# Down-projections of a squared-ReLU MLP as seven block products instead of eight, with their weight sums formed in HBM by the DMA queue

## The chip, the cores and the metric

The kernel runs on one core of one Trainium2 chip, as one launch. The metric is the device time of a launch in microseconds (us), the median of several runs. In the profile PE is TensorE, DVE is VectorE, ACT is ScalarE, POOL is GpSimd and SP is SyncE.

## What is computed

One layer of a hybrid decoder for 1088 tokens (a prompt of 1024 and 8 samples of 8): token mixers, cross-attention, then the MLP to which the change belongs, and a final norm. All is in float32.

```python
hm = _rmsnorm(x, g_mlp)
x = x + jnp.square(jax.nn.relu(hm @ w_up)) @ w_down   # (T, 1024) @ (1024, 4096), then (T, 4096) @ (4096, 1024)
y = _rmsnorm(x, g_final)
```

## The kernel before

**Number format.** Each float32 operand of a large product is kept as a high part (rounded to the matmul's format, fp32r) and a low part (the rest), and each product is three matmuls: high by high, high by low, low by high. Of every weight tile POOL makes the high part (the cast at L509, `msp<-mraw`) and DVE the low part (`unit_lo`, `msp<-mraw,msp`). Of the activations ACT makes the high part and DVE the low part.

**The MLP.** The hidden width of 4096 is worked through in eight stretches (d = 0, 1 of four groups o). A stretch has two quads (q) of 256 hidden rows each: the up-projection of a quad, and after both the down-projection of their 512 hidden rows into all 1024 outputs, which is added to the residual `F`. The first group and the last are written out, the middle two are a loop of two trips (`pair_loop`, L410).

**A quad** is already a block product with seven multiplications (`ORDER`, `PRODUCTS`): a product is 24 matmuls of 272 columns (`product`, L1293), its weight tile is one unit of 128x512 (an up-block of `w`, or a sum of blocks from the tensor `sums_up` in HBM). DVE combines the results (`Quad.c11`, `c22`, `c12`, `c21`), applies ReLU and scale (`squeezed`), ACT squares (`squared`) and makes the high part, DVE the low part (`hidden_lo`). The first stretch has an order of its own (`opening`).

**A down-projection** (`down`, L1368) has 8 output tiles of 128 rows, one weight unit each. A tile is 4 (contraction) x 3 (parts) x 3 (column pieces of 364, 364 and 360) = 36 matmuls, 288 in the stretch. Two sets of three PSUM banks take turns. DVE adds each tile to `F` in one instruction of 1092 columns.

**The weight sums.** Four sums per group (S1 to S4) for the up-projections are formed in HBM by DMAs that POOL issues, 32 steps of 1024 KB (`sum_step`, L471): `put` copies, `plus` adds while writing. One step follows each of the first 32 weight slots that POOL splits for the input projections (`split`, L442); slots 0 to 13 belong to the plain projections, slots 14 to 31 to the filling, where PE puts input-projection work between steps of the recurrence.

**What sets the order.** Every engine runs the order that its block writes out, tied by counting semaphores. In this program's rows some appear under the name of an earlier use: `as_tc` is m_used (PE has used a unit), `as_nm` is m_hi (POOL has cast a unit), `as_tp` is m_ready (its low part is there), `at_tc` is m_lo (low parts of the hidden activations), `at_ox` is m_f (reads of PSUM into `F`), `at_mx`, `at_ex`, `at_nm` are m_b, m_c, m_z (blocks of a quad), `at_tp` is m_sq (squares), `rg_t` is t_hi, `as_oc` is m_half, `o_dve` is DVE's wait for itself.

## Time and profile before

| | |
|---|---|
| median of 3 runs | 2252.41 us (2246.67 to 2255.57) |
| the profiled execution | 2245.91 us |
| its span, first to last instruction | 2244.1 us |
| PE busy | 2182.6 us (97%) |
| DVE busy | 1065.8 us (47%) |
| ACT, POOL busy | 533.4, 440.1 us |
| mean granted clock of PE | 0.996 |
| DMA queue of POOL (q0) | 12800 packets, 33.56 MB, 6.9% of 16 engines' span |

The span is divided into the input projections (to about 250 us), the recurrence with filling and the mixers, attention, and the MLP (from 1490 us to the end). Matmuls are pipelined in PE, so a matmul's own duration overlaps the next one; the spacing of starts is what it costs.

### The profile page before, as it was taken

The page shows a single profiled execution, that of the slowest core. Times are in us where ns is not written, and L with a number is a line of the kernel's source. Part 1 is how long each engine was busy: PE and PEld are TensorE (multiplying, and loading weights), DVE is VectorE, ACT ScalarE, POOL GpSimd, SP SyncE. Part 2 cuts the span into 40 slices and gives each one's busy share as a digit, 9 for nine tenths or more (in the row PEclk, how much of TensorE's full clock was granted, in tenths as well). Part 3 has the DMA queues.
Part 4 walks back from the last instruction along what each step waited for, and adds up shares of the span by engine and source line. Part 5 has one row for each costly group of instructions (what it writes and reads, how often), then busy time and mean ns, then how long its engine had stood idle before and what let it go on. Part 6 is the DMA issues. An engine that isn't in the chain of part 4 may idle for free. (4 is left out here: it accounts for less than half of the span.)

```text
span 2244.1 us, 49247 instructions
## 1 busy us (share of the span) xinstructions
PE 2182.6 (97%) x21418; PEld 2061.6 (92%) x21418; DVE 1065.8 (47%) x1526; ACT 533.4 (24%) x1014; POOL 440.1 (20%) x368
## 2 busy tenths in 40 slices
PE   8999999999999999999999999998999999999997
PEld 6899888888888899989999987998999999999997
DVE  5333643636445355263544155466445445354455
ACT  4111433324333221153011023231102011011023
POOL 0233301112021022122333200321111111111110
PEclk9999999999999999999999999999999999999999
DMA  8446513424053074336113125111212122122122
GB/s 306 144 129 137 142 39 82 89 54 149 7 114 70 27 244 162 105 135 254 47 40 119 47 96 187 38 57 62 70 53 76 57 67 72 52 76 64 55 76 80
DMA packets 86663, 217.61 MB, mean 97 GB/s; under 512 B 10720, under 2 KB 26464, under 8 KB 83680
## 3 DMA queue, kind: packets, MB, share of 16 engines
q1 hardware_dynamic: 62944, 156.22, 21.0%
q0 software_dynamic: 12800, 33.56, 6.9%
q10 hardware_dynamic: 10752, 25.35, 3.2%
q8 instruction: 137, 2.24, 0.4%
q14 instruction: 30, 0.25, 0.0%
HBM read 187.04 MB, written 61.60 MB: 111 GB/s over the span
## 5 line engine op out<-in xcount | busy, mean ns | idle before, releaser
L517 PE MATMUL ps<-A_s,w_split 128*128 128x364 f32 (+1 forms) x3888 | 693.5, 334 | 1.9 <-ACT zstg L2250 1.9
L517 PEld LDWEIGHTS ps<-A_s,w_split 128*128 128x128 f32 x3888 | 643.5, 188 | 28.1 <-issue 12.5
L517 PE MATMUL ps<-hid,msp 128*128 128x364 f32 (+3 forms) x2304 | 388.3, 330 | 5.4 <-issue 5.4
L517 PEld LDWEIGHTS ps<-hid,msp 128*128 128x128 f32 x2304 | 385.1, 189 | 7.3 <-issue 6.0
L449 POOL CAST w_split<-w_raw 128x1024 fp32r<-128x1024 f32 x78 | 85.5, 1096 | 1117.0 <-PE ps L517 858.0
L517 PE MATMUL ps<-B_s,w_split 128*128 128x364 f32 (+1 forms) x1728 | 288.1, 328 | 0.4 <-POOL w_split L451 0.4
L517 PEld LDWEIGHTS ps<-B_s,w_split 128*128 128x128 f32 x1728 | 286.7, 188 | 0.7 <-issue 0.7
L1434 DVE TENSOR_TENSOR F<-ps,F 128x1092 f32<-128x1092 f32 (+3 forms) x84 | 104.3, 1241 | 352.3 <-PE ps L517 352.3
L509 POOL CAST msp<-mraw 128x512 fp32r<-128x512 f32 x176 | 115.1, 655 | 616.6 <-PE ps L517 604.0
L451 POOL TENSOR_TENSOR w_split<-w_raw,w_split 128x1024 fp32r<-128x1024 f32 x78 | 206.9, 2652 | 6.3
L517 PE MATMUL ps<-xb,msp 128*128 128x272 f32 x1536 | 200.2, 288 | 1.5 <-DVE F L1434 1.5
L517 PEld LDWEIGHTS ps<-xb,msp 128*128 128x128 f32 x1536 | 195.9, 188 | 1.8 <-issue 1.8
L517 PE MATMUL ps<-xt,msp 128*128 128x272 f32 x1152 | 152.2, 288 | 1.5 <-DVE xt L1434 1.0
L517 PEld LDWEIGHTS ps<-xt,msp 128*128 128x128 f32 x1152 | 147.4, 188 | 2.1 <-DVE xt L1434 1.2
L1434 DVE TENSOR_TENSOR msp<-mraw,msp 128x512 fp32r<-128x512 f32 x176 | 121.2, 690 | 51.6 <-POOL msp L509 49.7
L2250 ACT ACTIVATE hidf<-ps 128x544 f32<-128x544 f32 x32 | 20.0, 626 | 383.2 <-PE ps L517 383.2
L1434 DVE TENSOR_TENSOR pdf<-prw 128x1024 f32<-128x1024 f32 x14 | 40.9, 2919 | 99.3 <-ACTq L2354 99.3
L2250 ACT ACTIVATE hid<-hidf 128x544 fp32r<-128x544 f32 x64 | 42.2, 660 | 190.9 <-DVE hidf L1440 190.9
L2250 ACT ACTIVATE zstg<-ps 128x364 f32<-128x364 f32 x96 | 45.3, 474 | 173.4 <-PE ps L517 130.0
L1434 DVE TENSOR_TENSOR hidf<-ps,hidf 128x544 f32<-128x544 f32 x62 | 44.9, 724 | 42.0 <-PE ps L517 42.0
L1434 DVE TENSOR_TENSOR Xst<-ps,msk 128x256 f32<-128x256 f32 (+1 forms) x88 | 35.8, 407 | 53.7 <-PE ps L517 52.0
L1434 DVE TENSOR_TENSOR F<-F 128x384 f32<-128x384 f32 (+2 forms) x64 | 43.9, 697 | 25.3 <-ACT F L2250 24.7
(249 smaller groups left out, 2408.4 us busy)
## 6 DMA issues: line engine op xcount, KB each, us to landing
w_raw<-w SPq DMA_DIRECT2D x80, 512.0 KB, 3.7
mraw<-w SPq DMA_DIRECT2D x112, 256.0 KB, 2.6
sums_up<-w POOLq DMA_DIRECT2D x24, 1024.0 KB, 9.4
mraw<-sums_up SPq DMA_DIRECT2D x64, 256.0 KB, 2.6
z<-zstg SPq DMA_DIRECT2D x83, 182.0 KB, 2.1
F<-z SPq DMA_DIRECT2D x16, 546.0 KB, 7.1
sums_up<-sums_up POOLq DMA_DIRECT2D x8, 1024.0 KB, 5.9
w_raw<-w SPq DMA_DIRECT2D x7, 1024.0 KB, 10.3
```

Of the source, the lines that this page charges most:

```text
L449: pool.tensor_copy(ws[:, b, 0, :, :], raw[:, b, :].rearrange("p (k n) -> p k n", k=KT)).then_inc(w_hi, 1)
L451: pool.tensor_tensor(ws[:, b, 1, :, :], raw[:, b, :].rearrange("p (k n) -> p k n", k=KT), w32, ALU.subtract).then_inc(w_ready, 1)
L509: pool.tensor_copy(msp[:, l % 4, 0, :, :], mraw[:, l % 4, :].rearrange("p (k n) -> p k n", k=4)).then_inc(m_hi, 1)
L517: return pe.matmul(out, lhsT, rhs, start=start, stop=stop, skip_group_check=skip)
L1434: return v.tensor_tensor(out, a, b, op)
L2250: return a.activation(out, in_, f, **k)
```

## The change

**Down-projections.** Six of the eight stretches, all but (o, d) = (0, 0) and (3, 1), take seven block products. The weight block is 1024 outputs x 512 hidden, cut in even and odd output tiles, two halves of 256 hidden rows (the two quads) and two halves of 544 tokens. A product has 4 output tiles, 2 contraction tiles, 3 parts and 2 column pieces of 272: 48 matmuls, 336 in the stretch. It takes two units (`FAST` lists 14), and each half of a unit's work ends in a tile that DVE reads into `F` (`read`, 544 columns, 28 a stretch). Four of the seven products use weight sums, from a new HBM tensor `sums_down`. The hidden operands must be combined too: `tf = H11 - H12`, `H12 - H22`, `tf + H22`, and two more, with their high parts by ACT (`turned_hi`) and low parts by DVE (`turned_lo`, `lower`). In these stretches DVE's low parts of 544 columns per quad are partly dropped and partly replaced.

**Residual.** Through these six stretches `F` holds its blocks in another basis; two DVE instructions of 2176 columns bring it in (after quad 2 of group 0) and two bring it back (after quad 2 of group 3): `residual_in`.

**Opening and first down-projection.** DVE's order at the end of `opening` is changed, and PE's first down-projection (`down_first`) goes through its first two tiles one contraction step at a time, with a wait for each.

**Weight sums.** 64 steps instead of 32, two after each of the first 32 slots. The 32 new ones form `sums_down`: 1024 KB in groups 1 and 2 (where a `plus` is two DMAs), 512 KB in groups 0 and 3. That makes 72 DMAs.

**Smaller edits.** A stretch has 14 units instead of 8; unit numbers run through the program (`mlp_units`, `mlp_ring`). One accumulator moves from banks 3 and 4 to banks 2 and 3. POOL's loop over slots is written out. SP's wait for all sums stands just ahead of the MLP's loads.

```diff
+        FAST = [(p, u) for p in (1, 2, 7, 3, 5, 4, 6) for u in range(2)]
+        UNITS_BEFORE, READS_BEFORE = {0: 0, 1: 50, 3: 162}, {0: 0, 1: 36, 3: 148}
+        def mlp_fast(o, d):
+            return (o, d) not in ((0, 0), (3, 1))
...
-            for n in range(XT + SIDE):
+            done = 0
+            for n in range(S_MLP - S_PW):
                 split(n, n % 2)
-                if n < 32:
-                    sum_step(n)
+                for _ in range(2 if n < 32 else 0):
+                    if done < 32:
+                        sum_step(done, 0, sum_block, up_block)
+                    else:
+                        sum_step(done - 32, 8, down_sum, down_block)
+                    done += 1
...
+            def down_first():
+                r = [mlp_ring(0, down_unit(0, 0, t)) for t in range(2)]
                 for t in range(2):
+                    pe.wait_ge(m_ready, mlp_units(0, 0, down_unit(0, 0, t) + 1))
+                    pe.wait_ge(m_lo, mlp_lows(0, 0, 0, 2))
+                    pe.wait_ge(m_b, BEFORE + 5 + t)
+                    down_part(r[t], t, (0,))
+                for k, n in ((2, 4), (1, 6), (3, 8)):
+                    pe.wait_ge(m_lo, mlp_lows(0, 0, 0, n))
+                    for t in range(2):
+                        last = down_part(r[t], t, (k,))
...
+            OPERAND = {1: (0, 0), 2: (1, 0), 7: (0, 1), 3: (1, 1), 5: (0, 0), 4: (1, 0), 6: (0, 0)}
+            NEED = {1: 1, 2: 3, 7: 4, 3: 6, 5: 5, 4: 7, 6: 8}
+            def down_fast(i, o, d):
+                n = 4 * o + 2 * d + 2
+                for s, (p, u) in enumerate(FAST):
+                    l = down_unit(o, d, s)
+                    v, h = OPERAND[p]
+                    if u == 0:
+                        pe.wait_ge(m_lo, mlp_lows(i, o, d, NEED[p]))
+                    pe.wait_ge(m_ready, mlp_units(i, o, l + 1))
+                    for j in range(2):
+                        t = 2 * u + j
+                        if s >= 2:
+                            pe.wait_ge(m_f, mlp_reads(i, o, d, 4 * (s // 2 - 1) + t + 1))
...
+                        for k in range(2):
+                            for m, (wp, xp) in enumerate(((0, 0), (0, 1), (1, 0))):
+                                for c in range(2):
+                                    x0 = HT * h + HC * c
+                                    last = mm(ps[:, 2 * t + c, 0:HC], msp[:, mlp_ring(o, l), wp, 2 * j + k, :], hid[v][:, k, xp, x0:x0 + HC],
...
+                        last.then_inc((m_half, m_used)[j], 1)
...
+            def down_fast(i, o, d):
+                for s, (p, u) in enumerate(FAST):
+                    l = down_unit(o, d, s)
+                    v.wait_ge(m_half, mlp_turns(i, o, d, 14, BEFORE + s + 1))
+                    read(p, 2 * u)
+                    v.wait_ge(m_used, mlp_units(i, o, l + 1))
+                    read(p, 2 * u + 1)
+                    unit_lo(i, o, l + 4)
+                    if s == 0:
+                        turned_lo(H12, 0, 1, mlp_turns(i, o, d, 4, BEFORE_R + 5))
+                    if s == 2:
+                        turned_lo(tf, 0, 0, mlp_turns(i, o, d, 4, BEFORE_R + 6))
+                    if s == 3:
+                        v.wait_ge(m_lo, mlp_lows(i, o, d, 5))
+                        own.add(tt(tf, H22, tf, ALU.add))
+                    if s == 4:
+                        own.wait()
+                        lower(1, 1)
+                    if s == 5:
+                        own.add(tt(H21_hi, f32(hid[1][:, :, 0, 0:HT]), tf, ALU.subtract))
+                    if s == 6:
+                        own.wait()
+                        tt(H21, H21_hi, f32(hid[1][:, :, 1, 0:HT]), ALU.add).then_inc(t_sum, 1)
+                    if s == 8:
+                        turned_lo(H21, 1, 0, mlp_turns(i, o, d, 4, BEFORE_R + 7))
+                    if s == 10:
+                        turned_lo(tf, 0, 0, mlp_turns(i, o, d, 4, BEFORE_R + 8))
```

DVE, a down-projection in the middle of the MLP, before: per weight unit one addition to `F` of 1092 columns and one low part.

```order
L1434 TENSOR_TENSOR hid_68<-hidf_70,hid_68 128x544 [waits at_tp]
L1434 TENSOR_TENSOR F<-ps,F 128x1092 [waits as_tc]
L1434 TENSOR_TENSOR msp<-mraw,msp 128x512 [waits as_nm]
```

The same place in the changed kernel, from the last low part of the second quad on (units s = 0 to 2 of 14).

```order
L1529 TENSOR_TENSOR hid_69<-hidf_71,hid_69 128x544 [waits at_tp]
L1529 TENSOR_TENSOR F<-F,ps 128x544 [waits as_oc]
L1529 TENSOR_TENSOR F<-F,ps 128x544 [waits as_tc]
L1529 TENSOR_TENSOR msp<-mraw,msp 128x512 [waits as_nm]
L1529 TENSOR_TENSOR hid_68<-hidf_70,hid_68 128x2x544 [waits rg_t]
...
L1529 TENSOR_TENSOR hid_68<-tf,hid_68 128x2x544 [waits rg_t]
...
L1529 TENSOR_TENSOR tf<-hidf_71,tf 128x1088 [waits at_tc]
...
L1529 TENSOR_TENSOR hid_69<-hidf_71,hid_69 128x2x544 [waits o_dve]
```

Per unit there are now two reads and one low part, and after eight of the units one more instruction of 1088 columns. The rows after units 0, 2, 3 and 4 are shown.

DVE at the end of the opening, before: from the fourth block of quad 1 (`c22`) to the third of quad 1 (`c21`). `hidf_70` and `hid_68` belong to quad 0, `hidf_71` and `hid_69` to quad 1.

```order
L1434 TENSOR_TENSOR hidf_71<-ps,hidf_71 128x544 [waits as_tc]
L1440 SCALAR_TENSOR_TENSOR hidf_71<-hidf_71,rsx 128x544 [waits at_mx]
L1434 TENSOR_TENSOR hid_68<-hidf_70,hid_68 128x544 [waits at_tp]
L1434 TENSOR_TENSOR hidf_70<-ps,hidf_70 128x544 [waits as_tc]
L1440 SCALAR_TENSOR_TENSOR hidf_70<-hidf_70,rsx 128x544 [waits at_mx]
L1434 TENSOR_TENSOR msp<-mraw,msp 128x512 [waits as_nm]
L1434 TENSOR_TENSOR hid_69<-hidf_71,hid_69 128x544 [waits at_tp]
L1434 TENSOR_TENSOR hid_68<-hidf_70,hid_68 128x544 [waits at_tp]
L1434 TENSOR_TENSOR hidf_71<-ps,hidf_71 128x544 [waits as_tc]
```

In the changed kernel:

```order
L1529 TENSOR_TENSOR hidf_71<-ps,hidf_71 128x544 [waits as_tc]
L1535 SCALAR_TENSOR_TENSOR hidf_71<-hidf_71,rsx 128x544 [waits at_mx]
L1529 TENSOR_TENSOR hid_68<-hidf_70,hid_68 128x544 [waits at_tp]
L1529 TENSOR_TENSOR msp<-mraw,msp 128x512 [waits as_nm]
L1529 TENSOR_TENSOR hid_68<-hidf_70,hid_68 128x544 [waits at_tp]
L1529 TENSOR_TENSOR hidf_70<-ps,hidf_70 128x544 [waits as_tc]
L1535 SCALAR_TENSOR_TENSOR hidf_70<-hidf_70,rsx 128x544 [waits at_mx]
L1529 TENSOR_TENSOR hidf_71<-ps,hidf_71 128x544 [waits as_tc]
```

The two low parts that stood ahead of the first row (and two between the rows) now come later, and the last row, which frees the PSUM banks of PE's second down tile, directly follows quad 0's.

## Rows read from the trace of the kernel before

**Rows 1.** The page: span, and busy time by engine.

```profile
span 2244.1 us, 49247 instructions
PE 2182.6 (97%) x21418; PEld 2061.6 (92%) x21418; DVE 1065.8 (47%) x1526; ACT 533.4 (24%) x1014; POOL 440.1 (20%) x368
```

**Rows 2.** The chain that ended last: start us, us, what.

```profile
1542.59 321.12 PE ps L517 x2160
1865.17 358.68 PE ps L517 x2466
```

**Rows 3.** Timeline of PE in the MLP: start us, us, instructions [idle before].

```profile
1533.94 3.28 PE L517 MATMUL ps<-xt,msp 128*128 128x272 f32 x24 [0.38 <-DVE hidf L1434]
1542.59 50.81 PE L517 MATMUL ps<-hid,msp 128*128 128x364 f32 x288 [5.37 <-issue]
...
1602.28 3.18 PE L517 MATMUL ps<-xb,msp 128*128 128x272 f32 x24
1605.29 3.18 PE L517 MATMUL ps<-xt,msp 128*128 128x272 f32 x24
...
1635.42 48.07 PE L517 MATMUL ps<-hid,msp 128*128 128x364 f32 x288
1683.33 6.19 PE L517 MATMUL ps<-xb,msp 128*128 128x272 f32 x48
```

**Rows 4.** Windows, two quads and the down-projection behind them: length, busy by engine, clock, DMA.

```profile
1593.20:1635.40 42.20, 42.20 (x338) 42.20 (x337) 25.76 (x37) 10.96 (x18) 8.83 (x14) 1.00 0.26 82
1635.40:1683.30 47.90, 47.90 (x290) 47.90 (x289) 16.67 (x19) 1.21 (x2) 4.94 (x8) 1.00 0.17 50
```

**Rows 5.** Timeline where a down-projection begins (PE's first matmul at 1635.42).

```profile
1635.62 0.72 DVE L1434 TENSOR_TENSOR hidf<-ps,hidf 128x544 f32<-128x544 f32 x1 [0.29 <-PE ps L517]
1635.74 0.62 POOL L509 CAST msp<-mraw 128x512 fp32r<-128x512 f32 x1 [2.40 <-PE ps L517]
1636.38 0.72 DVE L1440 SCALAR_TENSOR_TENSOR hidf<-hidf,rsx 128x544 f32<-128x544 f32 x1
1637.03 0.72 DVE L1434 TENSOR_TENSOR hid<-hidf,hid 128x544 fp32r<-128x544 f32 x1
1637.14 0.66 ACT L2250 ACTIVATE hid<-hidf 128x544 fp32r<-128x544 f32 x1 [1.81 <-DVE hidf L1440]
1637.66 0.68 DVE L1434 TENSOR_TENSOR msp<-mraw,msp 128x512 fp32r<-128x512 f32 x1
1637.71 0.64 ACT L2250 ACTIVATE hidf<-hidf 128x544 f32<-128x544 f32 x1
```

**Rows 6.** Timeline of the opening's end, where DVE and POOL are both busy.

```profile
1526.13 2.42 DVE L1434 TENSOR_TENSOR xt<-xtf,xt 128x2176 fp32r<-128x2176 f32 x1
1527.33 1.69 POOL L509 CAST msp<-mraw 128x512 fp32r<-128x512 f32 x1 [2.40 <-PE ps L517]
1528.47 1.10 DVE L1434 TENSOR_TENSOR msp<-mraw,msp 128x512 fp32r<-128x512 f32 x1
...
1533.17 0.71 DVE L1434 TENSOR_TENSOR hidf<-ps,hidf 128x544 f32<-128x544 f32 x1
1533.71 0.62 POOL L509 CAST msp<-mraw 128x512 fp32r<-128x512 f32 x1 [2.28 <-PE ps L517]
1533.91 0.99 DVE L1440 SCALAR_TENSOR_TENSOR hidf<-hidf,rsx 128x544 f32<-128x544 f32 x1
```

**Rows 7.** Timeline of POOL in a slot of the plain projections.

```profile
169.08 1.28 POOL L469 DMA_DIRECT2D sums_up<-w  x1 [0.73 <-POOL w_split L451]
176.78 1.04 POOL L449 CAST w_split<-w_raw 128x1024 fp32r<-128x1024 f32 x1 [6.42 <-issue]
```

**Rows 8.** Windows of 12 us (one slot): a copying step, then an adding one.

```profile
142.00:154.00 12.00, 12.00 (x74) 12.00 (x73) 4.54 (x4) 1.73 (x7) 4.19 (x4) 1.00 0.39 131
154.00:166.00 12.00, 12.00 (x74) 12.00 (x73) 4.54 (x4) 1.73 (x7) 4.76 (x4) 1.00 0.66 131
```

**Rows 9.** The page: a DMA queue (packets, MB, share), and issues with us to landing.

```profile
q0 software_dynamic: 12800, 33.56, 6.9%
...
w_raw<-w SPq DMA_DIRECT2D x80, 512.0 KB, 3.7
...
sums_up<-w POOLq DMA_DIRECT2D x24, 1024.0 KB, 9.4
```

More of the change, by code:

```diff
@@ L1360, in down_part @@
                         for c in range(3):
-                            last = mm(down_bank(t, c), msp[:, l % 4, wp, k, :], hid[k // 2][:, k % 2, xp, real(c)],
-                                      start=(k == m == 0), stop=(k == 3 and m == 2), skip=True)
-                return last
-            def down(i, o, first, d, tiles):
-                z0, f0 = 16 * o + 8 * d, 16 * o + 8 * d
+                            last = mm(G[t % 2][:, c, 0:real(c).stop - real(c).start], msp[:, r, wp, k, :],
+                                      hid[k // 2][:, k % 2, xp, real(c)], start=(k == m == 0), stop=(k == 3 and m == 2), skip=True)
@@ L2183, in quad @@
+                if odd:
+                    hidden_lo(i, z0, q, 0, 0)
                 unit_lo(i, o, l0 + 9)
+                if odd:
+                    squares_of(i, z0 + 3)
+                    tt(H12, H12, H22, ALU.subtract).then_inc(t_sum, 1)
                 c.c21()
-                hidden_lo(i, z0 + 2, q, 0, 1)
+                if alone:
+                    hidden_lo(i, z0 + 2, q, 0, 1)
                 unit_lo(i, o, l0 + 10)
-                hidden_lo(i, z0 + 3, q, 1, 0)
-            def down(i, o, d, tiles, last):
-                f0 = 16 * o + 8 * d
+                if alone or odd:
+                    hidden_lo(i, z0 + 3, q, 1, 0)
@@ L2192, in down @@
+            def down(o, d, tiles):
                 for t in range(tiles):
[L2193 to L2194 removed]
+                    l = down_unit(o, d, t)
+                    v.wait_ge(m_used, mlp_units(0, o, l + 1))
                     tt(tri(F[:, t, 0:T + 4]), G[t % 2], tri(F[:, t, 0:T + 4]), ALU.add).then_inc(m_f, 1)
[L2196 to L2197 removed]
@@ L2201, in pair_of_groups, with residual_in @@
+            F12, F21, F22 = F[:, 0:8:2, HT:T], F[:, 1:8:2, 0:HT], F[:, 1:8:2, HT:T]
+            def residual_in(n, op1, op2):
+                v.wait_ge(m_f, n)
+                own.add(tt(F12, F12, F22, op1))
+                own.add(tt(F21, F21, F22, op2))
+                own.wait()
             def pair_of_groups(i, o, first, last):
@@ L2205, in pair_of_groups @@
                         opening()
-                    else:
-                        quad(i, o, 2 * d)
-                        quad(i, o, 2 * d + 1)
-                    down(i, o, d, 6 if last and d == 1 else 8, last)
-            QUAD_STEPS = 1
+                        down(0, 0, 8)
+                        continue
+                    quad(i, o, 2 * d)
+                    if first:
+                        residual_in(mlp_reads(0, 0, 1, 0), ALU.add, ALU.subtract)
+                    if last and d == 1:
+                        residual_in(mlp_reads(0, 3, 1, 0), ALU.subtract, ALU.add)
+                    quad(i, o, 2 * d + 1)
+                    if mlp_fast(o, d):
+                        down_fast(i, o, d)
+                    else:
+                        down(3, 1, 6)
+            PAIR_STEPS = 10
             pair_of_groups(0, 0, True, False)
-            with v.Fori(0, 2) as i, own.loop(i, 2, 4 * QUAD_STEPS):
+            with v.Fori(0, 2) as i, own.loop(i, 2, PAIR_STEPS):
                 pair_of_groups(i, 1, False, False)
```

333 lines of the change are left out of this document (211 added, 122 removed).

## The prediction

> **What bounds the kernel now.** I read the page first. It should show one engine that never rests: PE is busy 97% of the span and every other engine 47% or less [rows 1]. The chain that ended last then says whether PE waits for anyone. From 1542.59 us on it is two runs of PE, 321.12 and 358.68 us, with 1.4 us between them [rows 2]. So the MLP costs what its matmuls cost, and fewer matmul columns shorten it one for one, as long as nobody becomes late.
>
> The timeline of PE gives the prices. A product of 24 matmuls of 272 columns takes 3.01 us (1602.28 to 1605.29), 125.5 ns each, 0.461 ns a column. A down-projection of 288 matmuls takes 47.91 us (1635.42 to 1683.33), 166.4 ns each, 0.459 ns a column of its mean 362.7 [rows 3]. Short matmuls thus cost no extra per column. The clock is at its full level, 2.4 GHz, in both [rows 4]. One place is different: before the first down-projection PE stands 5.37 us [rows 3].
>
> DVE, the second engine, is busy 25.76 us of 42.20 in two quads and 16.67 of 47.90 in a down-projection [rows 4]. That is the room the change will use.
>
> **The change, part by part.**
>
> *Matmuls.* Six stretches go from 288 x 166.4 ns = 47.91 us to 336 x 125.5 ns = 42.18 us: 5.73 us each, **34.4 us** in all. The two other stretches keep their matmuls.
>
> *DVE in such a stretch.* Prices are start to start. A 544-column instruction takes 0.63 us (1637.03 to 1637.66), 0.76 if it needs the result of the one ahead (1635.62 to 1636.38), and a unit's low part 0.61 (its 0.68 less the same overlap) [rows 5]. The 2176-column one took 2.34 us (1526.13 to 1528.47) [rows 6]. On the line between 544 and 2176 columns, 1088 columns cost 1.20 us. A unit then costs 2 x 0.65 + 0.61 = 1.91 us of PE's 3.01, and 3.11 with one of the eight new large instructions. Together 14 x 1.91 + 8 x 1.20 = 36.3 us of 42.2. It fits on average. What counts is where the large ones stand.
>
> Let D be the start of the stretch on PE, and the units end at D + 3.01, 6.03, 9.04, 12.05, 15.07, 18.08 and so on. When does DVE arrive? In the kernel before it reads the quad's last product 0.20 us after D, ReLU follows at 0.76, ACT squares until D + 2.9, and the last low part ends at D + 3.7 [rows 5]. Now H12 - H22 stands ahead of that read, and waits for ACT's square of the block before. The preceding block is itself later, because `tf` and `lower` (1.20 each) were put ahead of it: I get its ReLU ending at D - 1.1, the square at D + 0.1, H12 - H22 at D + 1.4, and the last low part at **D + 4.8**. Units 0 to 4 carry four large instructions, the last of which, `lower(1, 1)`, is the operand of PE's unit 6: 4.8 + 3.11 + 1.91 + 3.11 + 3.11 + 3.11 = D + 19.1, where PE wants it at D + 18.1. PE waits 1.1 us.
>
> *POOL against DVE.* The rows show more. POOL's cast of a unit takes 0.62 us and comes 0.32 us after PE has left the old one [rows 5]. In the opening one such cast began at 1527.33, inside DVE's 2176-column instruction, and took 1.69 us: it ended at 1529.02, about 0.6 us after that instruction. DVE's next one, begun at 1528.47, took 1.10 us instead of 0.68. A cast that began while DVE read PSUM kept its 0.62, and the SBUF-only instruction behind it took 0.99 instead of 0.72 [rows 6]. So a collision costs DVE 0.27 to 0.42 us. In units 1 to 4 of the new stretch DVE runs without a pause and is at a low part or a large instruction when the cast comes: four collisions, 1.5 us, plus 0.1. PE's wait grows to **2.7 us**. I take this value, and bound it by 1.1 (no collision) and 4.0 (DVE arrives 1.3 us later still). After it the later operands come about 0.2 us before they are wanted, and reads of PSUM have 4.5 us. Six stretches: **+16.2 us** (0 to 24). The Trainium skill, SBUF — State Buffer, section Who interferes with whom, says that a DVE instruction with two SBUF inputs contends with a GpSimd instruction that reads SBUF, and its section on two separate sides that the loser blocks for the whole instruction. By that rule the sum is -34.4 + 16.2 for this part, by DVE's own durations alone -34.4 + 6.6. The trace agrees with the rule in the cases above.
>
> *Opening and first down-projection.* Before, PE's last product of the opening began late, at 1533.94, when the read at 1533.17 freed its bank [rows 3, 6], and the down-projection began at 1542.59, after eleven more DVE instructions. In the new order that read stands two low parts earlier, about 1532.5, and PE ends the product at 1536.3. PE's first tile then wants quad 0's last block (1536.9), the second tile quad 1's (1538.4, seven instructions behind the read plus a collision), and the third piece a low part at 1540.4. Each piece is 9 matmuls, 1.5 us, so the first two tiles end near 1549.4 instead of 1542.59 + 12.0 = 1554.6. **-5.1 us** (-6.2 to -3).
>
> *Weight sums.* POOL's queue moved 33.56 MB in 6.9% of 2244 us, 155 us of all 16 engines [rows 9]; the new steps add 25.2 MB, some 116 us. In the first 16 slots there are now two 1024 KB steps per slot of 11.95 us. With a copying step the engines are 39% busy in 12 us, with an adding one 66%; loads of a slot's weights (512 KB) are in both [rows 8]. At about a third of the copying window for the load (1.6 us), an adding step takes 6.3 us, and two with a load 14.2 us against 11.95: in the four slots where `sums_up` gets its first additions the queue falls 9 us behind, and catches up in the next two. POOL itself has 6.42 us of rest before a slot's cast behind a 1.28 us issue [rows 7] and gets 2 us more to do. It waits only for steps issued 24 us or more earlier. Weight loads stand in another queue and land in 3.7 us, while they have about 20. What hides it all is PE's slot of 11.95 us; without it a slot would pay about 2.2 us. I take **+0.5 us** (-0.5 to +9).
>
> *Small ones.* `residual_in` is 2 x 2.34 us on DVE between two quads; DVE is then free from 2.2 us (group 0) or 3.7 us (group 3) after the quad's start, and the first thing that must come, the read of product 6, is at 9.2 us: hidden. If DVE were not free, PE would pay up to 4.7 us once. ACT's four large high parts are 1.2 us each in an engine that is busy 1.21 us of 47.90 [rows 4]. SP's loads become 14 instead of 8 a stretch and are asked for 9 us ahead. The loop's step costs what it did.
>
> **Sum.** -34.4 + 16.2 - 5.1 + 0.5 = **-22.8 us** against 2245.9 us, so 2223.1 us. That execution was 6.5 us below the median of the three runs; the same difference from 2252.4 gives **2229.6 us**. What a measurement of this kernel can tell from no change is about 0.5%, 11 us.
>
> **Rivals.**
> - *A: DVE keeps up.* Collisions are rarer, or DVE arrives sooner. For it: 14 casts of 0.62 us are a small share, and DVE is busy on average 86%. Against it: the order of units 2 to 6. At 1.1 us or less a stretch the change is -34.4 + 3 (0.5 a stretch) - 5.1 = -36 to -33 us: 2216 to 2220 us.
> - *B: DVE becomes the bound.* If every one of 14 casts costs 0.4 us and dependent pairs cost more, DVE needs 36.3 + 5.6 + 4.8 (arrival) = 46.7 us a stretch. Gain 1.2 x 6 + 5.1 = 12 us: 2240 us.
> - *C: slower, by the weight sums.* If an addition in the queue lands more than 30 us after its issue (now 9.4 [rows 9]), POOL stands at its wait with the next split behind it, and PE opens its slot late. From there each slot pays. All 116 us extra would cost, a half is +58 us: 2252.4 - 23.3 + 58 = 2287 us; the break-even is one fifth. For it: a pair of adding steps and a weight load fill more than a slot, 14.2 us of 11.95. Against it: a pair of copying steps needs some 8 us, so the backlog ends after two slots, and in the filling the slots are longer.
> - *D: short matmuls aren't cheap here.* A unit now has two waits and two signals. If a half unit of 12 matmuls took 0.1 us more, 28 x 6 x 0.1 = +17 us: 2246 us. Against it: products in the quads signal every 24 matmuls and keep exactly 3.01 us.
>
> **How the numbers follow.** Forecast (1.5 to 4 us of waiting a stretch) 0.50, A 0.22, B 0.14, C 0.06, D 0.08. The forecast's own range is 2221 to 2240. The range takes in A and most of B: 2212 to 2244 us. Faster by over 0.5%: all of the forecast and of A, over half of B, a part of D, 0.87. Within 0.5%: 0.09. Slower by over 0.5%: C less its mild cases, 0.04.
>
> **What would show it.** PE's stretches of 272-column matmuls on `hid` should span 44 to 46 us in the six stretches, with one gap of 2 to 3 us, 18 us in, released by DVE `hid`, and none behind it longer than 0.5. DVE instructions on SBUF alone beside POOL's `msp` casts should show means above 0.72 (544 columns) and 1.3 us (1088). The first down-projection should begin near 1537 in pieces. The time at which the MLP begins (1490 us before) tells the price of the sums: the same within 1 us. I am wrong if the stretches show no gap, or if the gaps stand at PSUM reads all through them, or if the MLP begins over 5 us later.

## The result, and the profile after

The changed kernel takes **2267.05 us** (median of 7 runs, 2261.03 to 2272.16) against 2252.41 us (7 runs, 2246.67 to 2259.08): a ratio of **1.0064**, 95% interval 1.0042 to 1.0085, so 0.6% slower where I forecast 2229.6 us. The prediction was wrong. Its profiled execution took 2272.16 us.

The page of the changed kernel, with the line that answers to [rows 1] and the queue line of [rows 9]:

```profile
span 2270.3 us, 50369 instructions
PE 2170.4 (96%) x21706; PEld 2044.3 (90%) x21706; DVE 1200.4 (53%) x1716; ACT 552.7 (24%) x1026; POOL 529.2 (23%) x444
...
q0 software_dynamic: 27840, 58.72, 13.2%
...
sums_up<-w POOLq DMA_DIRECT2D x24, 1024.0 KB, 8.8
```

PE is busy 12.2 us less and yet the span is 26.2 us longer: PE waits. Where? The timeline of PE in the MLP (start us, us, instructions; in brackets the idle time before and what ended it):

```profile
1540.19 6.19 PE L564 MATMUL ps<-xb,msp 128*128 128x272 f32 x48
...
1587.43 3.39 PE L564 MATMUL ps<-hid,msp 128*128 128x364 f32 x18 [0.47 <-DVE hidf L1529]
1591.02 45.36 PE L564 MATMUL ps<-hid,msp 128*128 128x364 f32 x270 [0.20 <-DVE hid L1529]
1636.21 6.19 PE L564 MATMUL ps<-xb,msp 128*128 128x272 f32 x48
...
1678.40 18.32 PE L564 MATMUL ps<-hid,msp 128*128 128x272 f32 x144
1698.22 24.51 PE L564 MATMUL ps<-hid,msp 128*128 128x272 f32 x192 [1.50 <-DVE hid L1529]
1722.57 6.19 PE L564 MATMUL ps<-xb,msp 128*128 128x272 f32 x48
...
1764.76 18.22 PE L564 MATMUL ps<-hid,msp 128*128 128x272 f32 x144
1785.16 26.33 PE L564 MATMUL ps<-hid,msp 128*128 128x272 f32 x192 [2.18 <-DVE hid L1529]
```

The MLP's first product stands at 1540.19; in the kernel before it is at 1489.79. From there to the end of the span it is 730.1 us against 754.3 (this length is called the MLP length below). So the MLP gained **24.2 us** (predicted: 34.4 - 16.2 + 5.1 = 23.3), and everything ahead of it lost **50.4 us** (predicted: 0.5). The first down-projection begins in pieces (a piece of 18 matmuls at 1587.43, 0.47 and 0.20 us of waiting). The stretches look as forecast: one gap 18 us in, released by DVE's `hid`, 1.50 to 2.18 us in the six.

PE's longest waits ahead of the MLP (waited for: us in total, times, longest). The changed kernel, 0 to 1540 us:

```profile
PE ps L564 <- issue: 21.8, 11, 4.0
PE ps L564 <- POOL w_split L481: 12.4, 5, 6.1
```

The kernel before, 0 to 1490 us:

```profile
PE ps L517 <- issue: 3.3, 4, 1.3
...
PE ps L517 <- POOL w_split L451: 0.4, 1, 0.4
```

`w_split` is the split weight that POOL hands to PE in every slot. So POOL is late. PE's timeline has two of these waits in the input projections, where PE of the kernel before has no rest from 68 to 247 us:

```profile
160.91 13.84 PE L564 MATMUL ps<-A_s,w_split 128*128 128x364 f32 x72 [6.14 <-POOL w_split L481]
178.23 49.58 PE L564 MATMUL ps<-A_s,w_split 128*128 128x364 f32 x288 [3.47 <-POOL w_split L481]
```

Such a rest costs more than its own length. The 72 matmuls that begin at 160.91 took 13.84 us at a mean granted clock of 0.87; at the full level, 2.4 GHz, 72 cost 12.0. Ahead of the MLP PE is busy 1466.9 us for the matmuls that took 1449.5 in the kernel before: 17.4 of the 50.4 us are the same matmuls run slower (mean granted clock of the changed kernel's executions 0.984 to 0.990, of the profiled one before 0.996), 33.0 are more standing of PE. The timeline of POOL from slot 4 on, where the additions begin, says at what POOL is late:

```profile
106.01 1.04 POOL L479 CAST w_split<-w_raw 128x1024 fp32r<-128x1024 f32 x1 [6.33 <-issue]
...
110.22 1.28 POOL L501 DMA_DIRECT2D sums_up<-w  x1 [0.69 <-POOL w_split L481]
119.83 1.27 POOL L501 DMA_DIRECT2D sums_up<-w  x1 [8.33 <-issue]
120.59 1.56 POOL L479 CAST w_split<-w_raw 128x1024 fp32r<-128x1024 f32 x1
...
128.84 1.25 POOL L501 DMA_DIRECT2D sums_up<-w  x1 [4.22 <-issue]
137.62 1.26 POOL L501 DMA_DIRECT2D sums_up<-w  x1 [7.53 <-issue]
138.37 1.55 POOL L479 CAST w_split<-w_raw 128x1024 fp32r<-128x1024 f32 x1
```

Read the third row, the second addition, against [rows 7]. The second addition of a slot is issued 9.61 us after the first, with 8.33 us of standing in between. The standing is at the issue itself: in the instruction order this second DMA has no wait for a semaphore (only the first of the pair has). The time fits the landing of the first: the DMA issued at 110.22 landed after 9.3 us, at 119.5, and the second was issued at 119.83 (8.8 us is the median in the page). Two additions then cost 2 x 8.8 = 17.6 us of POOL in a slot of 11.95, and the casts of slots 5, 6 and 7 stand at 120.59, 138.37 and 156.01: 17.7 us apart. POOL falls 5.8 us further behind in each such slot. Over the program this is how much later POOL's cast of a slot begins than in the kernel before (starts from the timelines of both, differences taken):

| slot | 4 | 5 | 6 | 7 | 8 | 15 | 18 | 22 | 27 | 33 | 48 | 72 |
|---|---|---|---|---|---|---|---|---|---|---|---|---|
| us later | 1.0 | 3.6 | 9.4 | 15.1 | 21.1 | 21.0 | 18.0 | 43 | 42 | 44.5 | 50.4 | 50.4 |

Most of it comes in two climbs. The first is the additions to `sums_up` in slots 4 to 7. The second, in slots 21 to 32, is those to `sums_down`, up to four DMAs in a slot (from slot to slot the lateness goes up and down there). A last 5.8 us come between slots 36 and 40, after the last sum; a smaller loss stands in the same place in experiment 8, and its cause stays open. My theory after this: **POOL's queue has room for less than two adding DMAs, and POOL stands at the next issue until the one ahead has landed.** The rivals: the transfers themselves are too much for the DMA engines (my own worry in the prediction), or landing waits (rival C).

### The profile page after: what moved, and what is told of

Read it like the earlier page. It is cut to its first block and busy times, and to the rows that moved or that the text cites. A ratio compares the mean times of both kernels' runs of the same rounds, so it can differ in the third digit from the quotient of the medians.

```text
span 2270.3 us, 50369 instructions
## 1 busy us (share of the span) xinstructions
PE 2170.4 (96%) x21706; PEld 2044.3 (90%) x21706; DVE 1200.4 (53%) x1716; ACT 552.7 (24%) x1026; POOL 529.2 (23%) x444
## 5 line engine op out<-in xcount | busy, mean ns | idle before, releaser
L564 PE MATMUL ps<-A_s,w_split 128*128 128x364 f32 (+1 forms) x3888 | 698.8, 335 | 18.2 <-POOL w_split L481 11.8
L564 PE MATMUL ps<-hid,msp 128*128 128x272 f32 (+4 forms) x2592 | 358.8, 300 | 11.4 <-DVE hid L1529 11.0
L564 PEld LDWEIGHTS ps<-hid,msp 128*128 128x128 f32 x2592 | 353.1, 190 | 16.3 <-issue 10.2
L556 POOL CAST msp<-mraw 128x512 fp32r<-128x512 f32 x212 | 164.7, 777 | 543.4 <-PE ps L564 530.6
L1529 DVE TENSOR_TENSOR msp<-mraw,msp 128x512 fp32r<-128x512 f32 x212 | 149.4, 707 | 57.0 <-POOL msp L556 54.2
L1529 DVE TENSOR_TENSOR F<-F,ps 128x544 f32<-128x544 f32 x168 | 115.2, 713 | 23.5 <-PE ps L564 22.9
L1529 DVE TENSOR_TENSOR F<-ps,F 128x1092 f32<-128x1092 f32 (+3 forms) x36 | 42.0, 1168 | 158.0 <-PE ps L564 158.0
L2424 ACT ACTIVATE hid<-hidf 128x544 fp32r<-128x544 f32 (+1 forms) x64 | 47.6, 744 | 288.6 <-DVE hidf L1535 173.2
L1529 DVE TENSOR_TENSOR pdf<-prw 128x1024 f32<-128x1024 f32 x14 | 27.4, 1957 | 118.3 <-ACTq L2528 118.3
L1529 DVE TENSOR_TENSOR F<-F 128x384 f32<-128x384 f32 (+3 forms) x68 | 52.6, 788 | 24.7 <-ACT F L2424 24.2
```

What stands on the lines that cost most here:

```text
L556: pool.tensor_copy(msp[:, r, 0, :, :], mraw[:, r, :].rearrange("p (k n) -> p k n", k=4)).then_inc(m_hi, 1)
L564: return pe.matmul(out, lhsT, rhs, start=start, stop=stop, skip_group_check=skip)
L1529: return v.tensor_tensor(out, a, b, op)
L2424: return a.activation(out, in_, f, **k)
```

## Experiments

All ratios are to the kernel before, in runs on the same chip; the experiments ran on several chips, and the medians of the kernel before range from 2248.0 to 2252.4 us, so a difference between medians of different groups (1 to 4, 5 to 7, 8 and 9, 10, the changed kernel itself) can hold some 4 us of that. "MLP start" and "MLP length" are from the profiled execution, as above.

### 1. The sums alone

The kernel before with the 64 sum steps of the change, two per slot; the down-projections stay as they were. POOL's written-out loop over the slots comes with them.

```diff
-            for n in range(XT + SIDE):
+            for n in range(S_MLP - S_PW):
                 split(n, n % 2)
-                if n < 32:
-                    sum_step(n)
-            with pool.Fori(0, (S_MLP - S_MIX) // 2) as i:
...
+                for _ in range(2 if n < 32 else 0):
...
```

> The kernel before with the 64 steps of weight sums, two after each of the first 32 slots; the down-projections are as before, so the 32 new sums are formed and not used. Theory Q (the issue of a second adding DMA in a slot holds POOL, the split of the next slot stands behind it, PE opens the slot late): the whole loss lies here, the MLP begins near 1535 instead of 1490 us, the time is 2285 to 2300 us, and POOL stands 7 to 9 us before the second adding DMA of a slot. Rival M (the loss comes from the longer program or from the written-out loop of POOL as part of the other edits): the same loss only in part. If the sums cost nothing, 2252 us.

Measured: 2298.29 us against 2249.7, ratio 1.0209 (1.0192 to 1.0226). MLP length 752.9 us, as before; MLP start 1526.55, 36.8 later, in a profiled execution that at 2281 us was some 17 us shorter than the median. The whole loss lies ahead of the MLP and comes without one of the new matmuls: by the medians 48.6 us. The written-out loop stays in every later run, also in those that lose little, so it is not the cause.

### 2. One DMA per slot

```diff
             for n in range(S_MLP - S_PW):
                 split(n, n % 2)
-                for _ in range(2 if n < 32 else 0):
+                next(steps, None)      # 72 DMAs, one per slot, slots 0 to 71
```

> The changed kernel with its 72 DMAs of weight sums one after each of the first 72 slots instead of two steps after each of 32. The bytes and DMAs are the same. Theory Q: POOL is never held for more than 1 us at an issue, the MLP begins at 1490 us plus or minus 4, the time is 2222 to 2236 us. Rival T (what costs is the traffic itself, which makes loads of weights and stores of results late): the MLP still begins 10 us or more late, since the same 59 MB are moved; 2240 us or more. Rival W (POOL waits for sums to land): no wait is left here either, so as Q.

Measured: 2244.12 us, ratio 0.9973 (0.9962 to 0.9984); MLP start 1513.72, length 730.3. A miss: I expected the start within 4 us of 1490 and 2222 to 2236 us, and by its numbers this run is on rival T's side (10 us or more late, 2240 or more). The casts split it. Up to slot 31 they are at most 1.9 us late, but there one DMA a slot is just what the kernel before does (the 32 DMAs of `sums_up`), so this part says only that one DMA at a time holds nobody; it does not acquit the bytes. The new DMAs stand in slots 32 to 71. In slots 51 to 71 they cost 0.6 us. In slots 36 to 50 they stand beside a loss of 18 us (casts 2.9 us late in slot 33, 5.3 in slot 36, 23.3 from slot 51 on). There POOL waits for weights, which land in 25.4 us (median of the issues between 804 and 876 us) against 14.3 in the kernel before. POOL's timeline:

```profile
841.47 1.09 POOL L479 CAST w_split<-w_raw 128x1024 fp32r<-128x1024 f32 x1 [13.12 <-DMA w_raw<-w]
...
860.73 1.04 POOL L479 CAST w_split<-w_raw 128x1024 fp32r<-128x1024 f32 x1 [13.08 <-DMA w_raw<-w]
```

### 3. More room in the queue, nothing else

```diff
-    nc = ...Bacc(..., dynamic_dma_scratch_size=2048)
+    nc = ...Bacc(..., dynamic_dma_scratch_size=2304)
```

> The changed kernel with one number changed: the memory for POOL's DMA queue is 2304 bytes a partition instead of 2048. Theory Q in its sharper form (the queue has room for not quite two adding DMAs of 512 rows): with an eighth more room the second adding DMA of a slot is issued without the 7 to 9 us of standing, at least where the queue was empty before; the MLP begins 10 to 35 us earlier than in the changed kernel (where it begins at 1540), the time falls to between 2232 and 2257 us. Rival T (traffic) and rival W (POOL waits for sums to land): the standing and the time stay as they are, 2267 us.

Measured: **2236.74 us**, ratio 0.9937 (0.9914 to 0.9959); MLP start 1502.58, length 729.7. One number takes 30.3 us off the changed kernel by the medians, some 29 by the ratios. Bytes, DMAs and slots are the same, so this is the run that acquits the bytes for most of the loss. POOL's timeline in slots 4 and 5, same instructions as above:

```profile
106.09 1.04 POOL L479 CAST w_split<-w_raw 128x1024 fp32r<-128x1024 f32 x1 [6.20 <-issue]
...
110.38 2.58 POOL L501 DMA_DIRECT2D sums_up<-w  x2 [0.76 <-POOL w_split L481]
118.05 1.04 POOL L479 CAST w_split<-w_raw 128x1024 fp32r<-128x1024 f32 x1 [5.09 <-issue]
...
124.74 2.54 POOL L501 DMA_DIRECT2D sums_up<-w  x2 [3.18 <-issue]
```

The pair goes out in one piece, and the next cast is at 118.05, on time. The queue does fall behind here: the pairs of slots 4 to 7 go out at 110.38, 124.74, 139.45 and 155.00, 14.4 to 15.6 us apart, behind 3.18 to 9.48 us of standing, the casts of slots 8 and 9 are 3.6 and 7.0 us late, and that of slot 10 is back at 1.1. PE's cover of a slot absorbs it. This is the backlog that the prediction had worked out (14.2 us for two additions and a load, 9 us behind, then caught up), and it was not the limit. The MLP still begins 12.8 us later than in the kernel before: casts are 10.8 us late in slot 32, behind the slots with three and four DMAs. And a wait for a sum to land would not go with more room, so rival W (waits for landings) falls.

### 4. DVE's large instructions one unit earlier

```diff
-                    if s == 2:
+                    if s == 1:
                         turned_lo(tf, 0, 0, mlp_turns(i, o, d, 4, BEFORE_R + 6))
-                    if s == 3:
+                    if s == 2:
...
-                    if s == 4:
+                    if s == 3:
```

> The changed kernel with three of DVE's large instructions in a fast stretch one unit earlier: the low part of tf after unit 1 instead of 2, tf + H22 after unit 2 instead of 3, the low part of H22 after unit 3 instead of 4. If PE's gap 18 us into each stretch (1.5 to 2.2 us) is the wait for that last low part, it ends 1.9 us earlier: gaps of 0 to 0.5 us, the time 8 to 11 us less, 2257 us. If the gap has another cause (the reads of PSUM, a weight unit), it stays and the time is 2267 us.

Measured: 2258.49 us, ratio 1.0053 (1.003 to 1.0077); MLP start 1533.54, length 721.3, 8.8 us shorter than in the change. The ratio alone does not tell it from the change (1.0042 to 1.0085); the MLP length does. The gap 18 us in is gone; PE's timeline has two small ones at reads of PSUM:

```profile
1671.81 12.31 PE L564 MATMUL ps<-hid,msp 128*128 128x272 f32 x96
1684.35 6.31 PE L564 MATMUL ps<-hid,msp 128*128 128x272 f32 x48 [0.23 <-DVE F L1529]
1690.88 24.56 PE L564 MATMUL ps<-hid,msp 128*128 128x272 f32 x192 [0.22 <-DVE F L1529]
1715.28 6.19 PE L564 MATMUL ps<-xb,msp 128*128 128x272 f32 x48
```

From 1671.81 to 1715.28 is 43.47 us, against 42.18 of pure matmuls in the prediction.

### 5. Sums placed by hand, at the old room

Experiment 4, with the 72 DMAs one or two per slot in chosen slots: copies in pairs or alone, additions one per slot, none in slots 35 to 40 and 48 to 50.

```diff
+            PLACES = {**{n: 2 for n in (0, 1, 2, 3, 12, 13, 18, 19, 24, 29, 51, 52, 59, 60)}, **ADDS(4, 12), **ADDS(14, 18),
+                      **ADDS(20, 24), **ADDS(25, 29), **ADDS(30, 35), **ADDS(41, 48), **ADDS(53, 59), **ADDS(61, 67)}
...
+                for _ in range(PLACES.get(n, 0)):
+                    next(steps)
```

> The changed kernel with its 72 DMAs of weight sums placed: no two adding ones after one slot, pairs of copying ones where they were free, and none after slots 35 to 40 and 48 to 50, where the spread kernel lost 22 us (20 of them while the results of the side projections are loaded back); and with the three large instructions of DVE one unit earlier. If theory Q (POOL held at the issue) and the traffic in slots 35 to 50 are the whole of the loss, the MLP begins at 1491 plus or minus 3 us and takes 721 us: 2214 to 2224 us by the median. If the total traffic costs wherever it is put, the MLP begins at 1505 or later: 2235 us or more.

Measured: 2232.71 us, ratio 0.993 (0.9917 to 0.9943); MLP start 1510.12, length 722.0. A miss: I expected the start near 1491 and 2214 to 2224 us; the start is on the rival's side (1505 or later), the time between the two. POOL's casts were on time (1.5 us late) to slot 32, but 6.4 us late in slot 33, 16 in slot 38, 20.3 from slot 50 on. Leaving six slots free was not enough.

### 6. POOL's casts of these stretches on ACT

Experiment 5, with 14 casts per stretch moved from POOL to ACT, which is nearly idle there [rows 4].

```diff
+        def cast_by_act(o, l):
+            return (o > 0 and l < 4) or any(mlp_fast(o, d) and 4 <= l - down_unit(o, d, 0) < 18 for d in range(2))
...
                 for l in range(pair_units(o)):
+                    if cast_by_act(o, l):
+                        continue
...
+                        act(msp[:, r, 0, :, :], mraw[:, r, :].rearrange("p (k n) -> p k n", k=4), ACT.Copy).then_inc(m_hi, 1)
```

> The kernel of e5_placed with POOL's casts of the weight units in the fast stretches made by ACT. Theory of collisions (a POOL cast and a DVE instruction with two operands in SBUF hold each other up): in these stretches no DVE instruction on SBUF of 512 columns takes over 0.75 us and none of 1088 over 1.35 us (now up to 1.1 and 1.7), the stretches go from 43.5 to about 42.6 us, 3 to 7 us less in all. Rival (the long durations are DVE's own, or come from PE's or ACT's accesses): they stay, and the time is that of e5_placed.

Measured: 2225.09 us, ratio 0.9889 (0.9874 to 0.9904); MLP start 1509.96, length 714.0, 8.0 us shorter than in experiment 5 (I had expected 3 to 7). A stretch now runs without a gap:

```profile
1648.36 42.47 PE L578 MATMUL ps<-hid,msp 128*128 128x272 f32 x336
1690.66 6.19 PE L578 MATMUL ps<-xb,msp 128*128 128x272 f32 x48
```

It takes 42.30 us; the prediction had 336 x 125.5 ns = 42.18. DVE's groups of 1088 columns (`hid`, from 1700 us on; the changed kernel first, then experiment 6) show the collisions go. In experiment 5, which differs from 6 in the casts alone, the mean was 1385 ns:

```profile
L1529 DVE TENSOR_TENSOR hid<-hidf,hid 128x1088 fp32r<-128x1088 f32 x21 | 29.8, 1421 | 0.0
```

```profile
L1543 DVE TENSOR_TENSOR hid<-hidf,hid 128x1088 fp32r<-128x1088 f32 x20 | 25.7, 1284 | 0.0
```

### 7. Copies in place of additions

The changed kernel with every adding DMA made a plain copy, so this run leaves the sums out: `sums_up` and `sums_down` hold single blocks. Same DMAs, same rows, old room of 2048.

```diff
-                    pool.dma_start(x, y, accum_op=ALU.add).then_inc(d_sum[g], 16)
+                    pool.dma_start(x, y).then_inc(d_sum[g], 16)
```

> The changed kernel with every addition of the weight sums made a plain copy (the sums are left out, the bytes written and the number of DMAs are the same). Theory Q with room counted in entries of which an adding DMA takes about twice those of a copying one: POOL is held only at the second of two copies of 1024 rows, under 1 us at those of 512 rows; the MLP begins at 1492 to 1510 us; 2225 to 2245 us. Rival R (POOL is held by any second DMA after a slot, or by each until the one before has landed): the standing before the second DMA stays at 3 us or more everywhere, the MLP begins after 1515 us, 2245 us or more.

Measured: 2233.93 us, ratio 0.9936 (0.9921 to 0.995); MLP start 1502.84, length 728.4. POOL's timeline in slot 4, and two of the places where it stands:

```profile
109.04 1.48 POOL L501 DMA_DIRECT2D sums_up<-w  x2 [0.62 <-POOL w_split L481]
...
275.11 0.97 POOL L496 DMA_DIRECT2D sums_down<-w  x1 [0.83 <-POOL w_split L481]
283.25 0.96 POOL L496 DMA_DIRECT2D sums_down<-w  x1 [7.17 <-issue]
...
422.12 2.22 POOL L501 DMA_DIRECT2D sums_down<-w  x3 [0.63 <-POOL w_split L481]
431.48 0.74 POOL L501 DMA_DIRECT2D sums_down<-w  x1 [7.14 <-issue]
```

Two copies of 512 rows go out together, and so do three; the fourth stands (the expectation had under 1 us at every copy of 512 rows). Of copies of 1024 rows (of 1 KB) the second stands. So, by these rows, 2048 bytes a partition hold at least 1536 and less than 2048 rows copied, and less than 1024 rows added (the change, which stands at the second addition of 512): **adding takes more room per row than copying**, more than one and a half times as much. Rows count here, not bytes: three DMAs of 512 KB fit, and so do two of 1024 KB in rows of 2 KB, but not two of 1024 KB in rows of 1 KB.

The Trainium skill, DMA: Bandwidth & Descriptors, sections Terms and The descriptor swizzle, says that GpSimd writes 16-byte descriptors into rings in SBUF, and that a transfer to 128 partitions makes 8 read descriptors for each of the 16 engines, plus one for completion. An estimate from that page, if a row here counts like a partition there and an engine's reads have one partition's bytes to themselves: 2048 bytes are 128 descriptors; three copies of 512 rows are 3 x 33 = 99, four are 132; two of 1024 rows are 130. The Trainium skill's page Collectives: The Full Stack, section The bandwidth ceiling, says that an adding transfer has two reads a chunk: 65 for an addition of 512 rows, 130 for two, and 2304 bytes are 144. The rows of experiments 3 and 7 shown here agree with each of these counts. No page says that POOL stands when the room is full; the rows do.

The count is not the whole rule. In experiment 9, with 2304 bytes, a pair of additions goes out in one piece at 632.93, but of the additions at 655.89 and 664.38 the second stood 7.25 us, until the first had landed (8.2 us after its issue), though the pair before had landed over 10 us earlier. The same happens at 679.85 (6.69 us) and 814.87 (7.51 us). Why 130 of 144 fit once and not the other time stays open.

### 8 and 9. Where sums may stand

Experiment 6 with room 2304, and two placings of the 72 DMAs:

```diff
-            PLACES = {...}                                             # experiment 6
+            PLACES = {**{n: 2 for n in range(16)}, **ADDS(16, 31), **ADDS(51, 76)}   # 8: none in 31 to 50
+            PLACES = {n: 2 for n in range(36)}                                       # 9: two each in 0 to 35
```

> The kernel of the run before (placed sums, earlier large instructions, POOL's casts of the fast stretches on ACT) with more room in POOL's queue (2304 for 2048) and the 72 DMAs of the sums kept away from slots 31 to 50, where the side results are stored and the rope loads stand: two per slot in slots 0 to 15, one in 16 to 30, one in 51 to 75. Theory 1: the 17 to 20 us that the two placed versions lost between slots 32 and 50 come from sum DMAs beside those loads and stores. Then the MLP begins at 1491 to 1497 us, its length stays 714, and the time is 2206 to 2213 us. Theory 2: the loss does not depend on where the sums stand (the queue of POOL is late for its own later work, or the data is slower once more is moved): the MLP begins after 1505 us and the time is 2219 us or more.

> The same, but all 72 DMAs two per slot in slots 0 to 35, the plainest placing that more room in the queue allows. Theory 1: slots 0 to 30 cost nothing, the ten DMAs in slots 31 to 35 cost some part of what was lost there: 4 to 10 us behind the other run, the MLP begins at 1496 to 1505 us, the time is 2212 to 2221 us. Theory 2 (where the sums stand does not matter, only POOL's standing at an issue): as the other run within 2 us.

Measured, experiment 8: **2212.62 us**, ratio **0.9835** (0.9815 to 0.9855); MLP start 1496.73. Experiment 9: 2227.63 us, ratio 0.9902 (0.9884 to 0.992); MLP start 1510.31. Theory 1 holds for the first. For the second it holds in kind and fails in size: I expected the ten DMAs in slots 31 to 35 to cost 4 to 10 us; the MLP begins 13.6 us later than in experiment 8, 1.5 of them from before slot 31, and the time is 15.0 us more. In experiment 9 POOL's cast is 5.0 us late in slot 32, 8.5 in slot 33, 25.6 in slot 36. The windows over slots 37 and 38 (window; us, busy of PE, PEld, DVE, ACT, POOL; clock; DMA share; GB/s) in the kernel before, with no sum there:

```profile
828.00:840.00 12.00, 12.00 (x74) 12.00 (x74) 11.82 (x8) 1.43 (x3) 4.93 (x2) 1.00 1.03 293
840.00:852.00 12.00, 12.00 (x74) 12.00 (x73) 10.08 (x8) 1.43 (x3) 4.50 (x2) 1.00 1.03 352
```

And in experiment 9, with POOL's timeline in the same place:

```profile
828.00:840.00 12.00, 9.01 (x55) 8.71 (x53) 6.55 (x6) 1.43 (x3) 0.00 (x0) 0.99 1.10 299
840.00:852.00 12.00, 5.47 (x23) 5.47 (x24) 8.74 (x4) 0.00 (x0) 9.12 (x5) 0.58 1.05 275
```

```profile
820.32 1.26 POOL L505 DMA_DIRECT2D sums_down<-w  x1 [0.68 <-POOL w_split L484]
841.76 1.25 POOL L505 DMA_DIRECT2D sums_down<-w  x1 [20.18 <-issue]
```

The DMA engines are full here **already in the kernel before** (share 1.03), with the side results' loads and stores. An addition of 512 KB issued into this takes not 7.7 us, the median in the changed kernel, but, in experiment 9, 17.1 (median of the four issued in 804 to 876 us). The one issued at 820.32 took 21.1, and POOL stood 20.18 us at the next issue, until it had landed. PE rested 9.5 us for `w_split`, and its mean granted clock was 0.58 in that window.

Of the 7 us that experiment 8 still begins later than the kernel before, 3.4 come by slot 19 and 3.6 in slots 37 to 40, where no sum stands. There its weights land in 20.0 us (median, 804 to 876 us) with no sum beside them, so the 25.4 of experiment 2 against 14.3 is not all the sums' doing. That remainder is open. Experiment 8 changed room and placing at once; what placing alone is worth at 2304 is its difference to experiment 9.

### 10. The change as it is, only its sums mended

The changed kernel, down-projections untouched, with the room and the placing of experiment 8.

```diff
-                for _ in range(2 if n < 32 else 0):
+                for _ in range(PLACES.get(n, 0)):      # 2 in slots 0 to 15, 1 in 16 to 30, 1 in 51 to 75
...
-    nc = ...Bacc(..., dynamic_dma_scratch_size=2048)
+    nc = ...Bacc(..., dynamic_dma_scratch_size=2304)
```

> The changed kernel with its down-projections as they are (large instructions and POOL's casts where the change put them), and only the sums mended: 2304 of room for 2048, two DMAs per slot in slots 0 to 15, one in 16 to 30, one in 51 to 75. It is the change as my prediction took it, with sums that cost next to nothing. Theory (queue room, and no sums in slots 31 to 50): the MLP begins at 1495 to 1499 us and lasts 729 to 731, the span is 2224 to 2230, the time 2226 to 2234 us, against 2229.6 predicted. Rival (the down-projections as the change has them lose something outside the MLP that the two earlier runs of placed sums hid by gains): the time stays above 2238 us.

Measured: **2227.16 us**, ratio 0.9906 (0.9891 to 0.992); MLP start 1495.11. This is the kernel that the prediction described, with sums that nearly hide: 2229.6 was forecast, a ratio of 0.990. Part of the match is luck: the MLP begins 5.3 us later than before (0.5 was forecast), the opening gave 2.3 us more than forecast, and the kernel before ran at 2248.0 us there, against which the gain is 20.9 us for a forecast of 22.8. Only the placing differs from experiment 3: the MLP begins 7.5 us earlier.

## Why the prediction was wrong, point by point

| term of the sum | predicted | measured |
|---|---|---|
| matmuls, six stretches | -34.4 | -32 to -34 without a gap (experiment 6: 42.30 to 42.59 a stretch) |
| PE waits for DVE, six stretches | +16.2 | matmuls and waits together -16.6 against -18.2: the stretches take 44.17, 46.57, 44.79, 46.57, 44.67 and 44.13 us (from the third the loop's step of 1.74 is taken out; the kernel before has one of 1.48) |
| opening, first down-projection | -5.1 | -7.4 (start of MLP to second pair of quads, 103.44 to 96.02) |
| **weight sums** | **+0.5** | **+50.4** in the profiled execution (the slowest of the seven), 14.6 + 24.2 = 39 by the medians |
| small ones | 0 | -0.2 left over in the MLP (24.2 less 7.4 and 16.6) |

- **The step that failed is the term of the weight sums, taken as +0.5 us (-0.5 to +9).** It asked whether the DMA engines had the time (in slots 4 to 32 they had, experiment 3) and whether POOL's waits for a landing would stand (none did). It said that POOL "gets 2 us more to do". It did not ask what POOL does when the next DMA does not fit in its queue: POOL stood at the issue 6.7 to 9.8 us, about a landing, before the second addition of a slot. In the trace of before there was one sum step per slot and it landed in 9.4 us of 11.95 [rows 9]: **two were never in flight at once**. That row showed no room for a second one; I read it as a latency that nobody waits for.
- **Rival C** had the place, the sign and nearly the size (2287 us against 2267.05, +58 for the sums against +50.4), but another mechanism: a landing over 30 us after its issue, at the wait for it. POOL stood at the issue, at landings of 8.8 us, and two adding DMAs a slot were enough. At a chance of 0.06 it was held too cheap: the argument against it (backlog of engine time ends after two slots) was about another resource.
- **The opening** gave 7.4 us for 5.1. The forecast took the first two tiles of the kernel before at full clock (12.0 us from 1542.59). After its rest of 5.37 us that kernel's mean granted clock was 0.51 from 1542.59 to 1548.60, near the lower level of 1.2 GHz, and its 288 matmuls took 50.64 us for 47.91. The changed kernel, which rests 0.47 us there, had 1.00. The start itself came 5.6 us sooner (5.7 forecast).
- **Short matmuls** cost no extra (rival D falls): 42.30 us for 336 in experiment 6.
- **DVE's arrival.** The last low part was forecast at D + 4.8 and `lower(1, 1)` done at D + 20.8 with collisions. In the stretch that starts at D = 1764.76 the rows of DVE say 1769.5 and 1784.94: D + 4.7 and D + 20.2.
- **The gap's size**, 2.7 forecast, 1.5 to 2.2 measured. Fewer collisions cost DVE time than the four I took: three in that stretch, two in the first (D = 1678.40, gap 1.50). These are the ones of that stretch behind D + 5, DVE and POOL:

```profile
1771.17 0.74 POOL L556 CAST msp<-mraw 128x512 fp32r<-128x512 f32 x1 [2.43 <-PE ps L564]
1771.35 1.70 DVE L1529 TENSOR_TENSOR hid<-hidf,hid 128x1088 fp32r<-128x1088 f32 x1
1774.17 0.62 POOL L556 CAST msp<-mraw 128x512 fp32r<-128x512 f32 x1 [2.26 <-PE ps L564]
1774.24 1.09 DVE L1529 TENSOR_TENSOR msp<-mraw,msp 128x512 fp32r<-128x512 f32 x1
...
1777.12 1.28 DVE L1529 TENSOR_TENSOR hid<-tf,hid 128x1088 fp32r<-128x1088 f32 x1
1777.17 1.70 POOL L556 CAST msp<-mraw 128x512 fp32r<-128x512 f32 x1 [2.38 <-PE ps L564]
...
1780.16 1.78 POOL L556 CAST msp<-mraw 128x512 fp32r<-128x512 f32 x1 [1.29 <-PE ps L564]
...
1783.15 0.65 POOL L556 CAST msp<-mraw 128x512 fp32r<-128x512 f32 x1 [1.21 <-PE ps L564]
1783.25 1.69 DVE L1529 TENSOR_TENSOR hid<-hidf,hid 128x1088 fp32r<-128x1088 f32 x1
```

  In three of them DVE pays 0.4 us (1.70 for 1.28, 1.09 for 0.68); in two POOL does, 1.70 and 1.78 for 0.62 (DVE's instruction of 1088 columns beside the second began at 1780.18 and kept its 1.28). The six gaps sum to 10.8 us, between the 16.2 of the sum with four collisions a stretch and the 6.6 without one. Experiment 6, without POOL's casts, ran the stretches at 42.3 to 42.6 us against 43.5 to 44.0 in experiment 5: some 1.3 us each.
- **The waits' term came near by luck.** Matmuls and waits gave 16.6 us for a forecast of 18.2, but the gaps alone sum to 10.8 us, 5.4 less than forecast. What the sum left out is the clock: behind the gap of 1.50 us the last 192 matmuls of a stretch took 24.35 us at a granted clock of 1.00 (1698.22 to 1722.57), behind that of 2.18 they took 26.17 at a mean of 0.93 (1785.16 to 1811.33). In the two stretches with gaps of 2.15 and 2.18 us the rest thus cost 1.8 us more than itself.
- **Where the forecast placed its tests**: "I am wrong if ... the MLP begins over 5 us later" was the one that spoke. The others came out nearly as written: the gaps are 1.5 to 2.2 us for 2 to 3, two stretches take 46.57 us for 44 to 46, and DVE's instructions of 544 columns on SBUF alone kept a mean of 0.72 us, not above it, while those of 1088 went to 1.421.

## What to carry to other kernels

In this kernel a DMA cost POOL more than its issue time once the queue's room was used up: POOL stood until an earlier one had landed, and whatever is queued behind it (here the weights that PE waits for) was late. Before putting a second DMA in flight where the trace shows one, count rows and whether they are added or copied, and look for a place in the trace where two are in flight together; if there is none, price "the engine stands one landing" as a rival. And before moving transfers into a quiet-looking part, read the DMA share there: additions put just ahead of and into a share of 1.03 made the MLP begin 13.6 us later (experiment 9 against 8).

Of the two repairs, room (2304 for 2048) is the cheaper: some 29 us for one number. Room, placing and the two edits on DVE's and POOL's work together give 2212.62 us, 1.65% faster than the kernel before.

## What the runs showed of the hardware

- With 2048 bytes a partition of room POOL stood at the issue of a second adding DMA of 512 rows until the first had landed, 7.5 to 8.3 us in slots 4 to 7. With 2304 the pairs of these slots go out in one piece (experiment 3), though not every later pair does (7.25 us of standing at 664.38 in experiment 9). A copy of the same rows takes less room (experiment 7).
- PE that had rested could run slower afterwards, in the changed kernel: 72 matmuls in 13.84 us for 12.0 behind a rest of 6.14 us (mean granted clock 0.87), 192 in 26.17 us behind one of 2.18 (0.93), but 24.35 behind one of 1.50 (1.00).
- With the DMA engines full (share 1.05 to 1.10), additions of 512 KB, 7.7 us in the changed kernel, took 17.1 (experiment 9), and POOL stood 20.18 us at an issue behind one of 21.1.
- Moving casts from POOL to ACT freed DVE: the mean of its 1088-column instruction went from 1385 ns (experiment 5) to 1284 (experiment 6). In a collision either side can pay: in the rows above DVE paid 0.4 us in the three cases in which POOL's cast had begun 0.07 to 0.18 us ahead of it, and POOL paid 1.08 us where its cast began 0.05 us behind DVE's instruction, and 1.16 where it began 0.02 us ahead of it.
